# Expert lists placed by TensorE products and router logits as split fp32r products, with the last norms' roots on ScalarE

## The reference, cut to what matters

```python
x = x + merge_branches(a, b, ga, gb, w_out)          # width 1024 -> 1024
h = rms_norm(x, norm_ffn_g)
g_logits = h @ w_rg + b_rg                           # 4 groups
g_sel, g_prob = argmax(g_logits), softmax(g_logits)[g_sel]
e_logits = (h @ w_re + b_re)[group g_sel]            # 8 of 32 experts
top_v, top_i = top_k(e_logits, 2)
top_w = softmax(top_v) * g_prob                      # two weights per token
act = silu(h @ w_g[e]) * (h @ w_u[e])                # 1024 -> 128
out = sum over the two experts of top_w * (act @ w_d[e])
y = rms_norm(x + out, norm_final_g)
```

## Time and profile before

| what | value |
|---|---|
| median of 3 runs | 1339.54 us (1336.98 to 1339.65) |
| the profiled execution's own time | 1338.37 us |
| its span, first to last instruction | 1336.6 us |
| mean granted TensorE clock | 0.983 |
| busy share PE, DVE, ACT, POOL | 95%, 69%, 37%, 36% |
| chain that ended last, by engine | PE 78%, DMA 8%, POOL 5%, ACT 3%, DVE 3% |

### The profile page before, as it was taken

How to read it: one execution, slowest core, us unless ns; L and a number is a source line. 1 busy time by engine, 2 the same in 40 slices (tenths; PEclk the granted TensorE clock), 3 DMA queues, 4 the chain that set the end, 5 groups by cost and what they waited for, 6 DMA issues and landing times.

```text
span 1336.6 us, 21305 instructions
## 1 busy us (share of the span) xinstructions
PE 1264.2 (95%) x7533; PEld 1098.9 (82%) x7533; DVE 928.5 (69%) x2190; ACT 498.4 (37%) x1074; POOL 481.5 (36%) x768
## 2 busy tenths in 40 slices
PE   5999999999989999998999998999999979999985
PEld 5999999999979999997777766999788758877742
DVE  5665888888899998854777775342656558777636
ACT  5554222122212113224665553000422237665533
POOL 5801595968884116643000010210012234333314
PEclk9999999999999999998999999999999989999998
DMA  7201232121213221103000231843222258999757
GB/s 258 72 27 42 78 85 81 37 79 38 70 36 123 96 67 56 28 1 100 1 16 2 67 100 50 297 149 135 111 96 79 79 203 301 348 341 342 298 196 317
DMA packets 79312, 163.78 MB, mean 123 GB/s; under 512 B 12529, under 2 KB 47937, under 8 KB 78065
## 3 DMA queue, kind: packets, MB, share of 16 engines
q1 hardware_dynamic: 65121, 129.31, 28.4%
q0 software_dynamic: 12656, 27.62, 6.1%
q10 hardware_dynamic: 1440, 5.58, 1.1%
HBM read 137.81 MB, written 39.21 MB: 132 GB/s over the span
## 4 chain that ended last, share of the span: by engine, by line
PE 78%; DMA 8%; POOL 5%; ACT 3%; DVE 3%; issue 2%; SPq 1%; POOLq 0%; ACTq 0%; DVEq 0%
PE bank L876 11%; PE bank L875 11%; PE bank L877 11%; PE bank L1085 4%; DMA region_h<-in_wd 4%; PE bank L1160 3%; PE bank L1267 3%; PE bank L1154 3%; PE bank L1003 2%; PE bank L1067 2%; PE bank L1172 2%; PE bank L1171 2%; PE bank L1173 2%; DMA region_t<-ffn_input_scratch,small_i 2%; PE bank L1156 2%
## 5 line engine op out<-in xcount | busy, mean ns | idle before, releaser
L1858 DVE MAX8 small<-region_kv 128x8 f32<-128x272 f32 (+4 forms) x241 | 190.2, 828 | 47.6 <-DVE region_kv L1863 47.5
L875 PE MATMUL bank<-h_hi,w_hi 128*128 128x384 f32 (+1 forms) x576 | 196.1, 340 | 0.0
L876 PE MATMUL bank<-h_lo,w_hi 128*128 128x384 f32 (+1 forms) x576 | 196.1, 340 | 0.0
L1863 DVE MATCH_REPLACE8 region_kv<-small,region_kv 128x272 f32<-128x272 f32 (+4 forms) x241 | 195.5, 818 | 0.0
L877 PE MATMUL bank<-h_hi,w_lo 128*128 128x384 f32 (+1 forms) x576 | 194.4, 338 | 0.0
L2189 POOL TENSOR_TENSOR w_lo<-w_stage,w_hi 128x512 fp32r<-128x512 f32 x64 | 80.8, 1299 | 144.8 <-ACT w_hi L1371 144.7
L875 PE MATMUL bank<-w_hi,h_hi 128*128 128x256 f32 x448 | 128.9, 288 | 2.3 <-ACT region_q L1434 2.3
L877 PE MATMUL bank<-w_hi,h_lo 128*128 128x256 f32 x448 | 125.9, 281 | 0.0
L876 PE MATMUL bank<-w_lo,h_hi 128*128 128x256 f32 x448 | 125.9, 281 | 0.0
L877 PEld LDWEIGHTS bank<-h_hi,w_lo 128*128 128x128 f32 x576 | 108.7, 189 | 0.0
L876 PEld LDWEIGHTS bank<-h_lo,w_hi 128*128 128x128 f32 x576 | 108.2, 188 | 0.6
(11 more groups left out here) (328 smaller groups left out, 3114.5 us busy)
## 6 DMA issues: line engine op xcount, KB each, us to landing
w_stage<-in_w_in SPq DMA_DIRECT2D x72, 256.0 KB, 3.2
region_kv<-in_xa SPq DMA_DIRECT2D x16, 512.0 KB, 5.8
region_q<-in_wg SPq DMA_DIRECT2D x12, 512.0 KB, 7.1
region_q<-in_wu SPq DMA_DIRECT2D x12, 512.0 KB, 19.4
region_q<-in_wd SPq DMA_DIRECT2D x12, 512.0 KB, 22.8
region_w<-in_wg SPq DMA_DIRECT2D x10, 512.0 KB, 7.1
region_w<-in_wu SPq DMA_DIRECT2D x10, 512.0 KB, 19.5
region_w<-in_wd SPq DMA_DIRECT2D x10, 512.0 KB, 22.6
```

Of the source, the lines that this page charges most:

```text
L875: mm(out, st_hi(k), mv_hi(k), start=(k == 0), stop=False)
L876: mm(out, st_hi(k), mv_lo(k), start=False, stop=False)
L1858: nc.vector.max(m8[:, q, :], x).then_inc(dve_c, 1)
L1863: nc.vector.match_replace(x, m8[:, q, :], x, TAKEN).then_inc(dve_c, 1)
```

## The change

Five edits. (1) The transposed `x2` and the router weights (with the norm's gain folded in) are kept as high part and rest; `logits` becomes eight fp32r products with 80 columns (both weight parts, with zero columns as padding) and eight with 40. DVE gets `x2t_rest` for the rests, twice per tile, and an unpacking of the weights once. (2) The first 128 entries of all lists are made in PSUM: DVE writes, per tile and choice, the entry beside each one-hot column (`r_entry`) and a 128-wide comparison of the rank with 0..127 (`r_at_place`); PE's `listing(t)` adds their two float32 products into `bank[2]`, and DVE reads `heads`, `gidx` and the weights from there. The scatters to HBM stay for lists over 128 entries; the last tile's two are issued after the first three gathers. (3) The last tile's normed rows are made by POOL (times the gain) and ACT (times the root), and ACT issues their write. (4) The table for long lists is made after expert 0's weight rests, nobody waits for it ahead of the experts, SP's weight loads are placed anew and `WARM` is 5. (5) The final norm's root is ACT's Sqrt and DVE's reciprocal; odd tiles are squared and scaled from PSUM without the copy to SBUF.

```diff
-WARM = 14
+WARM = 5
...
             def logits(t):
-                pe.wait_ge(t7_evac, 2 * t + 2)
+                pe.wait_ge(t7_low, 2 * t + 1)
                 if t >= 2:
                     pe.wait_ge(pos_ready, t - 1)
+                if t == 0:
+                    pe.wait_ge(wr_split, 1)
                 for k in range(KD):
-                    last = mm(bank[t % 2][:, 0:NG + NE], x2T[:, k, :], wrout[:, k, :], start=(k == 0), stop=(k == KD - 1),
+                    if k == 4:
+                        pe.wait_ge(t7_evac, 2 * t + 2)
+                    mm(bank[t % 2][:, 0:2 * RC], x2T_hi[:, k, :], wr_parts[:, k, :], start=(k == 0), stop=False,
+                       skip_group_check=True)
+                for k in range(KD):
+                    if k == 4:
+                        pe.wait_ge(t7_low, 2 * t + 2)
+                    last = mm(bank[t % 2][:, 0:RC], x2T_lo[:, k, :], wr_parts[:, k, 0:RC], start=False, stop=(k == KD - 1),
                               skip_group_check=True)
                 last.then_inc(lg_done, 1)
 
...
+            def listing(t):
+                pe.wait_ge(list_ready, t + 1)
+                for q in range(2):
+                    last = mm(bank[2][:, 0:2 * NE], r_at_place[:, q, :], r_entry[:, t % 2, q, :], start=(t == 0 and q == 0),
+                              stop=(t == NT - 1 and q == 1), skip_group_check=True)
+                last.then_inc(listed, 1)
...
             for t in range(1, NT):
                 pe.wait_ge(m_high, t + 1)
                 pe.wait_ge(m_low, t + 1)
+                if t >= 3:
+                    listing(t - 3)
                 out_half(t, 0, 0, KD)
                 x2_trans(t - 1, 1)
-                k1 = 4 if t < NT - 1 else 1
+                k1 = 4 if t < NT - 1 else 2
                 out_half(t, 1, 0, k1)
                 if t >= 2:
                     rank(t - 2)
                 logits(t - 1)
                 if t == NT - 1:
-                    out_half(t, 1, k1, 6)
-                    k1 = 6
+                    out_half(t, 1, k1, 7)
+                    k1 = 7
                     rank(t - 1)
+                    listing(t - 2)
                 x2_trans(t, 0)
                 out_half(t, 1, k1, KD)
             x2_trans(NT - 1, 1)
             logits(NT - 1)
+            listing(NT - 2)
             rank(NT - 1)
+            listing(NT - 1)
             pe.wait_ge(pos_ready, NT)
-            mm(bank[2][:, 0:NE], onesb, onehots[:, NT, :], start=True, stop=True).then_inc(cnt_done, 1)
+            mm(bank[1][:, P:P + NE], onesb, onehots[:, NT, :], start=True, stop=True).then_inc(rank_done, 1)
...
                 else:
+                    act.wait_ge(rstd_ready, NT)
+                    act.wait_ge(h2_scaled, 1)
+                    nc.scalar.activation(h2_last, h2_last, ACT.Copy, scale=tnrm[:, NT - 1, 1:2]).then_inc(h2_ready, 1)
+                    act.wait_ge(h2_ready, NT)
+                    act.dma_start(h2_d[(NT - 1) * P:NT * P, :], h2_last).then_inc(h2_last_out, 16)
...
+            nc.scalar.activation(froot[:, NT, :], eps_col, ACT.Sqrt)
+            n_ms = 0
             for t in range(NT):
                 if t % 2 == 0:
                     act.wait_ge(y1_done, t // 2 + 1)
+                    nc.scalar.activation(fsq[:, t % 2, :], x2[:, t, :], ACT.Square, scale=1.0 / 32.0,
+                                         accum_out=fnrm[:, t, 0:1]).then_inc(fms_ready, 1)
+                    n_ms += 1
+                    offset = eps_col
                 else:
...
+                    for hf in (1, 0):
+                        act.wait_ge(y1_pe, t + 1 - hf)
+                        nc.scalar.activation(fsq[:, t % 2, hf * 512:(hf + 1) * 512], bank[t - 1 + hf][:, :], ACT.Square,
+                                             scale=1.0 / 32.0, accum_out=fnrm[:, t, hf:hf + 1]).then_inc(fms_ready, 1)
+                        n_ms += 1
+                        if hf == 1:
+                            act.wait_ge(fms_ready, n_ms)
+                            offset = fnrm[:, t, 1:2]
+                            nc.scalar.activation(offset, offset, ACT.Identity, bias=eps_col).then_inc(fms_ready, 1)
+                            n_ms += 1
+                act.wait_ge(fms_ready, n_ms)
+                nc.scalar.activation(froot[:, t, :], fnrm[:, t, 0:1], ACT.Sqrt, bias=offset).then_inc(frstd_ready, 1)
...
+            def x2t_rest(t, hf):
+                dve.wait_ge(t7_evac, 2 * t + hf + 1)
+                tt(x2T_lo[:, 4 * hf:4 * hf + 4, :], bank[6 + hf][:, :].rearrange("p (k t) -> p k t", k=4),
+                   x2T_hi[:, 4 * hf:4 * hf + 4, :].bitcast(F32), ALU.subtract).then_inc(t7_low, 1)
...
+                if t >= 2:
+                    dve.wait_ge(listed, t - 1)
+                for q in range(2):
+                    tt(r_entry[:, t % 2, q, :].rearrange("p (e w) -> p e w", w=2),
+                       r_oh[:, t, q * NE:(q + 1) * NE].unsqueeze(2).to_broadcast([P, NE, 2]),
+                       pairs[:, t, q, :].unsqueeze(1).to_broadcast([P, NE, 2]), ALU.mult)
...
+                if t >= 1:
+                    dve.wait_ge(listed, t)
+                for q in range(2):
+                    last = ts(r_at_place[:, q, :], place_iota, r_rank[:, t, q:q + 1], None, ALU.is_equal)
+                last.then_inc(list_ready, 1)
+                nc.vector.tensor_copy(entry_w[:, t, :, 1], pairs[:, t, :, 1])
...
+            link(nc.vector.tensor_copy(wr_parts[:, :, 0:NG], wrout[:, :, 0:NG]))
+            link(nc.vector.tensor_copy(wr_parts[:, :, 8:RC], wrout[:, :, NG:NG + NE]))
+            tt(wr_parts[:, :, RC:RC + NG], wrout[:, :, 0:NG], wr_parts[:, :, 0:NG].bitcast(F32), ALU.subtract)
+            tt(wr_parts[:, :, RC + 8:2 * RC], wrout[:, :, NG:NG + NE], wr_parts[:, :, 8:RC].bitcast(F32),
+               ALU.subtract).then_inc(wr_split, 1)
...
-            h2_of(NT - 1)
-
-            dve.wait_ge(cnt_done, 1)
-            for s in range(2):
-                dve.wait_ge(h2_out[s], 16 * ((NT - s + 1) // 2))
-            link(nc.vector.memset(f_one, 1.0))
-            link(nc.vector.tensor_copy(r_rb, bank[2][:, 0:NE]))
-            link(tt(f_flag, r_rb.unsqueeze(1).to_broadcast([P, OVER_J, NE]),
-                    overthr.unsqueeze(2).to_broadcast([P, OVER_J, NE]), ALU.is_gt))
-            link(nc.vector.tensor_tensor_scan(f_cum, f_one, f_flag.rearrange("p a b -> p (a b)"), 0.0, ALU.mult, ALU.add))
-            link(ts(f_junk, f_cum, siota, 0.0, ALU.is_le, ALU.add, accum_out=f_id))
-            link(nc.vector.tensor_copy(over_i[:, 0:1], f_id))
-            nc.vector.tensor_copy(over_i[:, 1:2], f_cum[:, NE * OVER_J - 1:NE * OVER_J]).then_inc(over_ready, 1)
-
-
-            dve.wait_ge(lidx_in, 16)
...
+            dve.wait_ge(listed, NT)
+            found = bank[2][:, 0:2 * NE].rearrange("p (e w) -> p e w", w=2)
+            link(ts(heads[:, :, 0], found[:, :, 0], float(SENT), None, ALU.add))
             ts(gidx, heads[:, :, 0], 1, None, ALU.logical_shift_right).then_inc(gidx_ready, 1)
+            nc.vector.tensor_copy(pos_w[:, :, 1], found[:, :, 1])
...
             expert_lower(0)
+            overflow_table()
+            rows_lower(0)
             expert_lower(1)
-            rows_lower(0)
...
                 dve.wait_ge(frstd_ready, t + 1)
-                stt(out=x2[:, t, :], in0=x2[:, t, :], scalar=fnrm[:, t, 1:2], in1=gfin,
-                    op0=ALU.mult, op1=ALU.mult).then_inc(fin_ready, 1)
+                link(nc.vector.reciprocal(froot[:, t, :], froot[:, t, :]))
+                if t % 2 == 0:
+                    stt(out=x2[:, t, :], in0=x2[:, t, :], scalar=froot[:, t, :], in1=gfin,
+                        op0=ALU.mult, op1=ALU.mult).then_inc(fin_ready, 1)
+                    return
+                for hf in range(2):
+                    cs = slice(hf * 512, (hf + 1) * 512)
+                    last = stt(out=x2[:, t, cs], in0=bank[t - 1 + hf][:, :], scalar=froot[:, t, :], in1=gfin[:, cs],
+                               op0=ALU.mult, op1=ALU.mult)
+                last.then_inc(fin_ready, 1)
...
+                if t == NT - 1:
+                    pool.wait_ge(x2_ready, 2 * NT)
+                    tt(h2_last, x2[:, t, :], gffn, ALU.mult).then_inc(h2_scaled, 1)
+                pool.wait_ge(ms_ready, t + 1)
+                rstd(tnrm, t).then_inc(rstd_ready, 1)
+            list_out(NT - 2)
...
-                if t == NT - 1:
-                    sp.wait_ge(o7_done, 2 * NT)
-                    load_e(3)
                 sp.wait_ge(h2_ready, t + 1)
-                sp.dma_start(h2_d[t * P:(t + 1) * P, :], h2[:, t % 2, :]).then_inc(h2_out[t % 2], 16)
-
-            sp.wait_ge(scattered, 16 * 2 * NT)
-            sp.dma_start(heads[:, :, :], lists[0:P, :, :]).then_inc(lidx_in, 16)
-            for e in range(4, NSLOT):
+                sp.dma_start(h2_d[t * P:(t + 1) * P, :], h2).then_inc(h2_out, 16)
+            sp.wait_ge(o7_done, 2 * NT)
+            sp.wait_ge(h2_out, 16 * (NT - 1))
+            load_e(3)
```

(60 more changed lines are left out.)

100 lines of the change are left out of this document (57 added, 43 removed).

## The result

The changed kernel takes 1325.56 us (median of 4 runs, 1325.06 to 1326.04), beside 1339.6 us for the kernel before on the same chip (4 runs, 1336.98 to 1340.09): a ratio of 0.9899, interval 0.9882 to 0.9916, some 14 us less. In three later series of runs the kernel before had medians of 1335.5 to 1336.2, and the changed kernel, run again in one of them (`e12_after_again`), took 1326.34 against 1336.04: 0.9935, interval 0.9920 to 0.9950, or 6.7 to 10.7 us. So it is faster in both. I had forecast 1332, within 1326.5 to 1337.5, which is a gain of 7.5: the direction was right and both times lie just under the range, but only the first ratio is clear of the forecast gain; the second one's interval holds it.

The account below looks back on a forecast made before the run. PE bounds the output projection, then a single hand-over chain on which the expert stage hangs; the tail is mixed. 3.3 + 1.05 - 8.25 - 1.5 - 1.5 = -6.9 from 1338.37 gives 1331.5, forecast 1332, range 1326.5 to 1337.5 us.

Parts of the forecast that it names:

- Router products, 0: Output projection loop on PE: sixteen records again at 0.11 us each, 1.8 us per tile, so no change.
- `listing`, +3.3: PE in the output projection: four records, 0.45 us a tile; seven tiles +3.15, plus 0.15 for waits.
- DVE's last tile, +1.05: Last tile's DVE queue: 1.76 us more ahead of the last residual addition, less 0.70 idle, delays it by 1.06 us.
- The hand-over, -8.25: From the last residual addition to expert 0's transposes: 17.4 us instead of 25.66, PE's ten constant records ending last.
- Expert 0's clock, -1.5: Expert 0's first 4.44 us, at clock 0.62 before, run at full clock: nearly all of 1.7 us saved.
- The tail, -1.5: Final norm: DVE's waits for POOL's root go, new DVE instructions come; middle of -2.4 and -0.6 us.
- The end, 0: From the last final to the end of the span: last landing taken as before, no change.
- More gain: Rival, chance 0.13: all constants at full clock, the tail's full 2.4 us and cheaper router products, 1322 to 1328 us.
- The late gather: Rival, chance 0.14: hand-over's gather takes 9.0 us, PE idles and the clock gain is lost; 1336 to 1337 us.
- DVE as the bound: Slower rival, chance 0.07: DVE passes 14.45 us per tile in the output projection loop, each us beyond costing eight.
- the head start: Rival, chance 0.08: transfers bound the expert stage, so placing weight loads later gives the saving back; 1337 to 1338 us.
- The lock of DVE and GpSimd: Last tile: DVE with two SBUF inputs and GpSimd exclude each other, so POOL's new product could be held up; unpriced.

Follow-up runs that it names:

- e12_after_again: The changed kernel as it is, run again in a later series beside the kernel before: 1326.34 us, 0.9935 of the kernel before.
- e1_tail_only: Kernel before with only the fifth edit (final norm's root on ACT and DVE, no POOL in the tail): 1330.37 us, 0.9955 of the kernel before.
- e2_pool_last: Changed kernel, with POOL writing one unread 128x1 constant after the last final: 1330.00 us, 0.9957 of the kernel before.
- e6_fp32_logits: Changed kernel with its first edit undone (router logits as eight float32 products of 40 columns, no rests): 1323.83 us, 0.9908 of the kernel before.
- e4_warm14: Changed kernel with 14 products of constants in the hand-over instead of 5: 1333.35 us, 0.9981 of the kernel before.
- e8_loads_first: Changed kernel without SP's wait for the first gather, so weight loads of slots 5 and 6 go ahead of it: 1329.78 us, 0.9948 of the kernel before.
- e9_root_early: Changed kernel with the last tile's root made earlier, ahead of POOL's 128x1024 product: 1325.95 us, 0.9932 of the kernel before.
- e10_before_warm5: Kernel before with 5 products of constants instead of 14: 1337.58 us, 1.0015 of the unaltered kernel before.
- e5_warm2: Changed kernel with 2 products of constants in the hand-over instead of 5: 1328.65 us, 0.9934 of the kernel before.

## Why the prediction was right and wrong

**What bounds the kernel.** Right for the loop and the hand-over. For the tail I followed the chain to the last `final`, at 1328.82 + 1.28 = 1330.1, and never asked what fills the 6.4 us from there to the end of the span, though SP has the last write after 2.7. With "PE's products and the last landing are as before" I put the end at nothing. This is the step that failed: the end of the kernel before was not the last write but POOL's drain, and with the roots off POOL these 3.2 us went (`e1_tail_only`), and came back with one late constant on POOL (`e2_pool_last`).

**Router products, 0.** Right: 0.92 + 0.88 us for the sixteen records, and `e6_fp32_logits`.

**`listing`, +3.3, and DVE's last tile, +1.05.** Together 4.35, measured 3.5. A `listing` in the loop is 0.39 us, and the tile grew by 0.44. The larger part is DVE: I had added `x2t_rest(7, 1)`, 0.69 us, to its queue, but it runs while `route(7)` waits for the logits (0.32 us of idle time were even left there), so `resid(8, 1)` kept PE waiting only a third of a us longer than before (1.22 for 0.88).

**The hand-over, -8.25.** Right in its mechanism, -9.0: `route(8)` at R + 3.5 (3.55), comparisons at R + 9.2 (9.4), gather 4.8 us (4.8), transposes at R + 16.6 (17.4). What was off is the ten records, 6.4 us for 6.8, and the `listing` ahead of them. The 4.46 us at half clock had the end of a window that I had read as their end; the clock was at 0.50 for the first 5.4 of the 14.95 us, which makes a record 0.44 and not 0.45, and in the changed kernel it rose after 3.9. That it reaches the end is shown by `e4_warm14`.

**Expert 0's clock, -1.5.** Right, 6.3 to 4.8 us. (PE's idle time behind the transposes was 0.8 us, not the 1.2 that I had read, and it is still there.) Behind it, over 31 experts, 0.9 us were given back, where I had taken the shift one to one. The same kernel's second profile has 188.1 for 188.9, so one pair of profiles shows no such thing; but all fourteen agree: with the first gate product at R + 18.2 to 19.6 this stretch takes 188.1 to 188.9 us (nine profiles), with it at R + 22.9 or later 186.9 to 188.0 (five). Transfers were at 0.85 of the stretch where they were at 0.83; that the weights' pace takes it is not shown.

**The tail, -1.5.** Mis-sized, -2.9 in the first profile and -2.6 in `e1_tail_only`, over my upper end of 2.4. I had the reciprocals at 0.2; they are 0.15, and the two halves of an odd `final` take 1.41 us together for 1.28 of one whole. With this DVE's `combine(8)` waits for its rows (0.4 us), and in the chain of waits transfers are the bound up to it and DVE behind it.

**The end, 0.** It was -3.2. With the tail the fifth edit is worth 6.1 of the 12.4 us of span; with the drain priced the forecast would have been 1329. The stretches miss the forecast by 5.5 us together: 3.2 here, 1.4 in the tail, 0.85 in the loop, 0.75 in the hand-over and 0.2 ahead of the stage, less the 0.9 given back.

**The rivals.** "More gain" (1322 to 1328) had 0.13 and holds the time, but of its three causes only the tail's was there; the constants were not all at full clock and the router products were not cheaper. So its range holds the time by luck: it lacks the drain. The late gather exists (`e8_loads_first`), and DVE as the bound does not, even with 11.5 us a tile. Of the head start under 1 us was given back.

**The lock of DVE and GpSimd,** which the Trainium skill (SBUF — State Buffer, the section on two separate sides) describes, did not matter: POOL's new product took 2.37 us beside the second `x2t_rest` with its PSUM input, for 2.41 in the earlier trace rows, and that `x2t_rest` took 0.69 us, as elsewhere.

## What to carry to other kernels

Read the span to its very end. Where the last engine or transfer record ends some us before the span does, as 3.6 us here, look for an engine that is still closing its list. Here it was POOL, and the fix was to give it no work in the last 7.5 us, not to speed up the chain. A wait that keeps weight loads behind one small gather can be worth more than the loads' head start, and constants on PE are worth keeping as long as they end about when what the engine waits for is there: later costs in full (`e4_warm14`), and 3 us earlier costs the clock, though 0.9 us earlier did not (`e9_root_early`, expert 0 in 4.8 us).

## What the runs showed of the hardware

POOL's closing drain ended 7.5 us behind POOL's last instruction in all fourteen profiles (7.51 to 7.53). Its record starts with that instruction, so it shows 7.6 us in the twelve where the last one is a constant of 0.1 us, and 8.1 and 9.0 us in the two where it is the last root, of 0.57 and 1.39 us (`before` and `e10_before_warm5`). The drains of PE (6.1 to 7.9 us), DVE (1.3) and ACT (0.3 to 2.1) ended 0.04 to 0.05 us behind their engine's last instruction in every profile: a long record there is unfinished work and costs nothing of its own.

Behind 3.1 us of idle time ahead of expert 0's transposes PE was at half its clock, and it was still there from 1088 to 1092 us, busy for all of it (`e5_warm2`); expert 0 took 6.8 us for 4.8. Behind 0.9 us it stayed at full clock (`e9_root_early`).
